# Gate and modulation applied by VectorE, the residual stream put into DRAM before the scatters, and a final norm tile by tile

## The reference

```python
hc, hl = rms_norm(x, norm2) * (1 + sc2) + sh2            # xc and xl, each with its own modulation
xc = xc + g2c * ec_moe(hc, ...)
xl = xl + g2l * ec_moe(hl, ...)
y_prompt, y_sample = rms_norm(xc, final_norm), rms_norm(xl, final_norm)

def ec_moe(x, w_router, w_gate, w_up, w_down):
    gate, idx = top_k(softmax(x @ w_router, over experts), cap)   # 64 latent + 16 context rows per expert
    xs = x[idx]
    y = (silu(xs @ w_gate) * (xs @ w_up)) @ w_down * gate
    return zeros.at[idx].add(y)
```

## Time and profile before

| what | us |
|---|---|
| timed runs | 1527.20, 1529.37, 1529.86; median 1529.37 |
| profiled execution, whole | 1521.83 |
| its span | 1520.0 |
| busy in the span | TensorE 1286.7 (85%), VectorE 890.7 (59%), ScalarE 754.6 (50%), POOL 183.9 (12%) |
| DMA | 322.33 MB, mean 212 GB/s |
| mean granted clock of TensorE | 0.931 of full speed |
| layer 1's expert stage | from about 1158 to 1486 us of the span |

### The profile page before, as it was taken

The page is one execution under the profiler, slowest core; times in us unless marked ns, Lnnn a source line. Parts: engine busy times, 40 slices in busy tenths (PEclk is TensorE's granted clock), DMA queues, the critical chain, the costliest instruction groups (busy, mean ns, idle before and its releaser), DMA issues.

```text
span 1520.0 us, 18235 instructions
## 1 busy us (share of the span) xinstructions
PE 1286.7 (85%) x7585; PEld 929.3 (61%) x7585; DVE 890.7 (59%) x1011; ACT 754.6 (50%) x876; POOL 183.9 (12%) x120
## 2 busy tenths in 40 slices
PE   5699978897679999999669998999953999899990
PEld 3579746795346555556449994668833655555650
DVE  2521367524668878778364352553257688778874
ACT  2321226613357777777243213553144677677762
POOL 1000010010012222211020000000101012222111
PEclk9879989998789999999779999899987999999995
DMA  6731056004699999999862311003054799999984
GB/s 237 236 111 56 28 198 221 2 28 176 231 311 338 364 361 365 363 360 356 285 194 84 97 61 53 2 1 112 2 230 139 275 361 364 360 350 364 369 288 147
DMA packets 98695, 322.33 MB, mean 212 GB/s; under 512 B 6239, under 2 KB 29998, under 8 KB 82230
## 3 DMA queue, kind: packets, MB, share of 16 engines
q1 hardware_dynamic: 86230, 278.39, 50.6%
q0 software_dynamic: 10272, 34.92, 8.6%
q10 hardware_dynamic: 2112, 7.87, 1.3%
HBM read 297.35 MB, written 23.81 MB: 211 GB/s over the span
## 4 chain that ended last, share of the span: by engine, by line
PE 50%; DMA 19%; DVE 16%; ACT 13%; issue 2%; DVEq 0%; ACTq 0%
PE psum L779 47%; DMA stage<-in_moe_w_gate 11%; DVE w_lo L1697 8%; ACT w_hi L1611 5%; ACT arena L1536 3%; DMA stage<-in_moe_w_up 2%; DMA stage<-in_w_mod 2%; DVE arena L1966 2%; ACT arena L1634 1%; DMA arena<-in_x_prompt 1%; DMA arena<-acc_dram 1%; ACT arena L1317 1%; DMA h_dram<-arena 1%; DMA stage<-in_ev_w_in 1%; DVE arena L1729 1%
## 5 line engine op out<-in xcount | busy, mean ns | idle before, releaser
L1697 DVE TENSOR_TENSOR w_lo<-stage,w_hi 128x2048 fp32r<-128x2048 f32 (+1 forms) x216 | 491.5, 2281 | 247.1 <-ACT w_hi L1611 139.9
L1611 ACT ACTIVATE w_hi<-stage 128x2048 fp32r<-128x2048 f32 x192 | 366.7, 1913 | 122.0 <-DMA stage<-in_moe_w_gate 58.1
L779 PE MATMUL psum<-w_hi,h_hi 128*80 128x512 f32 (+1 forms) x848 | 332.5, 392 | 55.1 <-DVE w_lo L1697 34.6
L779 PE MATMUL psum<-w_lo,h_hi 128*80 128x512 f32 (+1 forms) x848 | 326.6, 385 | 0.0
L779 PE MATMUL psum<-w_hi,h_lo 128*80 128x512 f32 (+1 forms) x848 | 326.5, 385 | 0.0
L779 PE MATMUL psum<-h_hi,w_hi 128*128 128x320 f32 x672 | 211.7, 315 | 4.2 <-DVE h_lo L1741 4.2
L779 PEld LDWEIGHTS psum<-w_hi,h_hi 128*80 128x80 f32 (+1 forms) x848 | 130.5, 154 | 135.7 <-DVE w_lo L1697 41.2
L779 PE MATMUL psum<-h_lo,w_hi 128*128 128x320 f32 x672 | 210.2, 313 | 0.0
L779 PE MATMUL psum<-h_hi,w_lo 128*128 128x320 f32 x672 | 210.0, 312 | 0.0
L779 PEld LDWEIGHTS psum<-w_hi,h_lo 128*80 128x80 f32 (+1 forms) x848 | 130.5, 154 | 63.9 <-issue 1.8
L779 PEld LDWEIGHTS psum<-w_lo,h_hi 128*80 128x80 f32 (+1 forms) x848 | 131.0, 154 | 53.6 <-issue 1.2
(11 more groups left out here) (224 smaller groups left out, 1218.6 us busy)
## 6 DMA issues: line engine op xcount, KB each, us to landing
stage<-in_moe_w_gate SPq DMA_DIRECT2D x64, 1024.0 KB, 8.9
stage<-in_moe_w_up SPq DMA_DIRECT2D x64, 1024.0 KB, 9.1
stage<-in_moe_w_down SPq DMA_DIRECT2D x64, 1024.0 KB, 6.6
stage<-in_w_mod SPq DMA_DIRECT2D x48, 1024.0 KB, 7.7
stage<-in_ev_w_in SPq DMA_DIRECT2D x7, 1024.0 KB, 9.4
stage<-in_od_w_in SPq DMA_DIRECT2D x7, 1024.0 KB, 7.7
acc_dram<-arena POOLq DMA_DIRECT2D x2, 2560.0 KB, 13.6
h_dram<-arena ACTq DMA_DIRECT2D x10, 512.0 KB, 3.0
```

The source lines that it names most:

```text
L779: return pe.matmul(o, w, x, start=first, stop=last, skip_group_check=True)
L1611: nc.scalar.activation(split_slot(w_hi, q0), stage[:, PIECE * (p0 % SLOTS):PIECE * (p0 % SLOTS) + PIECE], ACT.Copy)\
L1697: return nc.vector.tensor_tensor(dst, src, hi.bitcast(F32), ALU.subtract)
```

## The change

1. `acc_dram` of layer 1 is no longer cleared. ScalarE stores each `x_out` tile into it, and scatter 0 waits for these five stores.
2. TensorE turns the g2 block (128x16) once, ScalarE copies it and stores it to `gate_dram`, and POOL loads it back as rows: 64 partitions with the latent row, 16 with the context row. POOL also loads `final_norm` onto 128 partitions. Diagonals, spread matmuls and their evacuations go.
3. `rows_out` of layer 1 is VectorE's: one operation multiplies the 80x1024 PSUM result by the gate column and by the g2 row. It stands behind the split of u1, ahead of `hidden_split`; in the last expert behind d0 (expert 14) and at the end (expert 15).
4. At the end SP, not POOL, loads the five tiles, which are now already the sum. ScalarE squares tile t+1 before it makes the root of tile t; VectorE makes mean, Newton step and scaling tile by tile.

```diff
@@ plan_psum
         if L == LAYERS - 1:
+            one("gate rows", "act")
             for t in range(NT):
                 one(("x out", t), "act", 2)
...
-            for b in range(6):
-                one(("spread", b), "act")
@@ SyncE
+            sp.wait_ge(scattered, 16 * E * LAYERS)
+            for t in range(NT):
+                sp.dma_start(acc_out[t], acc_dram[LAYERS - 1][P * t:P * t + P, :]).then_inc(acc_out_in[t], 16)
             for t in range(NT):
                 sp.wait_ge(y_done, t + 1)
@@ GpSimd
-                    for layer in range(LAYERS):
-                        clear(layer)
-                    pool.wait_ge(zero_out, 16 * LAYERS)
+                    clear(0)
+                    pool.wait_ge(zero_out, 16)
...
+                if L == LAYERS - 1:
+                    emptied(pool, ("x out", NT - 1))
+                    pool.dma_start(gain_rows.rearrange("q (k p) -> q k p", k=KD),
+                                   a["final_norm"].rearrange("(o k p) -> o k p", o=1, p=P).to_broadcast([P, KD, P])).then_inc(gain_rows_in, 16)
+                    pool.wait_ge(gate_turned_out, 16)
+                    for rows, g in ((slice(0, CAP_L), 0), (slice(CAP_L, CAP), 1)):
+                        pool.dma_start(gate_rows[rows, :].rearrange("q (k p) -> q k p", k=KD),
+                                       gate_dram[:, g, :].rearrange("(o k) p -> o k p", o=1).to_broadcast([rows.stop - rows.start, KD, P]))\
+                            .then_inc(gate_rows_in, 16)
                 emptied(pool, (L, "gates"))
...
                     pool.wait_ge(y_ready, E * L + e + 1)
+                    if e == 0 and L == LAYERS - 1:
+                        pool.wait_ge(x_stored, 16 * NT)
...
-            for t in range(NT):
-                pool.dma_start(acc_out[t], acc_dram[LAYERS - 1][P * t:P * t + P, :]).then_inc(acc_out_in[t], 16)
@@ TensorE
                 if L == LAYERS - 1:
-
+                    emptied(pe, ("mod turned", LAYERS * MODS - 1))
+                    begin("gate rows")
+                    pe.transpose(bank("gate rows")[0:2 * KD, 0:P], mod_blocks_of(L, 5), ident).then_inc(psum_full, 1)
...
-                    pe.wait_ge(gain_diag_ready, 1)
-                    pe.wait_ge(gate_diag_ready, 1)
-                    for b in range(6):
-                        begin(("spread", b))
...
-                    emptied(pe, ("spread", 5))
-
+                    emptied(pe, ("x out", NT - 1))
@@ ScalarE
                 if L == LAYERS - 1:
+                    act.wait_ge(new_out, 16 * 4)
+                    evacuate("gate rows", gate_turned, bank("gate rows")[0:2 * KD, 0:P])
+                    emptied(act, "gate rows")
+                    act.dma_start(gate_dram.rearrange("k g p -> (k g) p"), gate_turned).then_inc(gate_turned_out, 16)
                     for t in range(NT):
                         evacuate(("x out", t), x_out[t], pair(("x out", t), n=D))
+                        emptied(act, ("x out", t))
+                        act.dma_start(acc_dram[L][P * t:P * t + P, :], x_out[t]).then_inc(x_stored, 16)
...
-                if L == LAYERS - 1:
-                    for b in range(6):
-                        evacuate(("spread", b), spread[:, 512 * b:512 * b + 512], bank(("spread", b)), scale=float(D))
...
                 def rows_out(e):
 
+                    if L == LAYERS - 1:
+                        return
...
+            def root_out_of(t):
+
+                act.wait_ge(mean_ready, t + 1)
+                nc.scalar.activation(root_out[:, t:t + 1], squares_out[:, t:t + 1], ACT.Ln).then_inc(log_done, 1)
+                logs[0] += 1
+                act.wait_ge(log_done, logs[0])
+                nc.scalar.activation(root_out[:, t:t + 1], root_out[:, t:t + 1], ACT.Exp, scale=-0.5).then_inc(root_done, 1)
+
             for t in range(NT):
...
+                act.wait_ge(acc_out_in[t], 16)
+                nc.scalar.activation(x_out[t], acc_out[t], ACT.Square, accum_out=squares_out[:, t:t + 1]).then_inc(x_squared, 1)
+                if t:
+                    root_out_of(t - 1)
+            root_out_of(NT - 1)
@@ VectorE
-                if L == LAYERS - 1:
-                    dve.wait_ge(roped, 8)
-                    for k in range(KD):
-                        ins = nc.vector.tensor_scalar(gain_diag[:, P * k:P * k + P], ident, cols[:, R_FIN + k:R_FIN + k + 1], None, ALU.mult)
...
-                            ins = nc.vector.tensor_scalar(gate_diag[:, at:at + P], ident, mod[:, L, 5, k, g:g + 1], None, ALU.mult)
...
+                def rows_out(e):
+
+                    if L < LAYERS - 1:
+                        return
+                    dve.wait_ge(moe_used, piece_number(e, "d1", 6 * n0 + 1))
+                    if e == 0:
+                        dve.wait_ge(gate_rows_in, 32)
+                    if e >= 2:
+                        dve.wait_ge(scattered, 16 * (n0 + e - 1))
+                    nc.vector.scalar_tensor_tensor(ysb[e % 2].rearrange("p (b n) -> p b n", b=2), psum[0:CAP, 6:8, :], gates[:, e:e + 1],
+                                                   gate_rows.rearrange("p (b n) -> p b n", b=2), ALU.mult, ALU.mult).then_inc(y_ready, 1)
+
                 def step(e, more=True):
                     expert_split(plus(e, 1), "u0")
                     expert_split(plus(e, 1), "u1")
+                    if e:
+                        rows_out(e - 1)
                     hidden_split(e)
...
+            dve.wait_ge(gain_rows_in, 16)
             for t in range(NT):
...
+                mean, root = squares_out[:, t:t + 1], root_out[:, t:t + 1]
+                dve.wait_ge(x_squared, t + 1)
+                nc.vector.tensor_scalar(mean, mean, 1.0 / D, EPS, ALU.mult, ALU.add).then_inc(mean_ready, 1)
+                roots[0] += 1
+                dve.wait_ge(root_done, roots[0])
+                newton(mean, root)
+                nc.vector.scalar_tensor_tensor(x_out[t], acc_out[t], root, gain_rows, ALU.mult, ALU.mult).then_inc(y_done, 1)
```

More of the change, by code:

```diff
@@ L471, in trunk @@
         squares_out, root_out = rowmax, rowsum
-        spread = xT_[:, 0:3 * D]
-        gate_diag, gain_diag = arena[:, 4096:4096 + 2 * D], cs[:, :]
+        gate_rows, gain_rows = xT_[0:CAP, 0:D], xT_[:, D:2 * D]
+        gate_turned = small[0:2 * KD, 0:P]
         consts_in, rows_in, x_in, router_in, sel_in, zeroed, zero_out = (
@@ L496, in trunk @@
         h_out = [sem(f"h_out{s}") for s in range(2)]
[L497 removed]
+        gate_turned_out, gate_rows_in, gain_rows_in, x_stored = (
+            sem(n) for n in ("gate_turned_out", "gate_rows_in", "gain_rows_in", "x_stored"))
         acc_out_in = [sem(f"acc_out_in{t}") for t in range(NT)]
@@ L1627, in rows_out @@
                 def rows_out(e):
+                    if L == LAYERS - 1:
+                        return
                     act.wait_ge(moe_used, piece_number(e, "d1", 6 * n0 + 1))
[L1630 to L1634 removed]
+                    if e >= 2:
+                        act.wait_ge(scattered, 16 * (n0 + e - 1))
+                    nc.scalar.activation(ysb[e % 2].rearrange("p (b n) -> p b n", b=2), psum[0:CAP, 6:8, :], ACT.Copy, scale=gates[:, e:e + 1])\
                         .then_inc(y_ready, 1)
@@ L2112, in _ @@
                 expert_split(E - 1, "d0")
+                rows_out(E - 2)
                 hidden_split(E - 1)
                 expert_split(E - 1, "d1")
+                rows_out(E - 1)
                 if L + 1 < LAYERS:
```

45 lines of the change are left out of this document (6 added, 39 removed).

## The result

Four runs of the changed kernel took 1511.96, 1512.96, 1504.87 and 1505.74 us, median 1508.85; four runs of the kernel before, on the same chip, have a median of 1529.45. The ratio is 0.9877, 95% interval 0.9845 to 0.9909: 18.8 us less (13.9 to 23.7). The forecast was 1513.6 in a range from 1507 to 1523. The profiled execution is one of the longer two, 1511.96 with a span of 1510.1, so the two traces show only 9.9 us of it. I take these apart first; what is missing comes at the end of the experiments. One execution of the kernel before, of 4370 us, stands apart from all its others (1515.6 to 1531.1) and is left out throughout.

A forecast was written before the change was run, and what follows sets the result against it. The weight stream (DMA 1.00 busy at 355 GB/s) was taken to bound the experts, TensorE just under it. Start −9.5, scaling 0, last expert +0.2 and +0.15, tail −6.7 made −15.8 from 1529.4: 1513.6 us, range 1507 to 1523.

The forecast's parts named there:

- The start: Layer 1's slots to first expert matmul: 9.4 us instead of 19.7, 10.3 gained, 9.5 net of slower first 36 matmuls.
- The yardstick from layer 0: Layer 0 starts the same experts without a spread, 9.4 us from slots to first matmul; taken for layer 1.
- What was put ahead of the gather: Ahead of gather 0, ScalarE's extra copy and issues and POOL's three broadcast loads were to cost 0.
- Rival 1: Layer 1's start: broadcasts hold up gather 0, TensorE starts 9 us later than forecast; gain 6.8, 1522.6 us; chance 0.10.
- So I put 0 on it: Expert stage: VectorE's row scaling, 1.25 us per expert, fits into its 1.59 us gap and costs 0.
- the forecast's own sign: First expert matmul to last scaling should take 306.9 + 1 us; over 310 means rival 2 is at work.
- rival 2: Expert stage: rows_out delays release of weight slots, 21.8 us paid, 6 us slower, 1535.4; decides from 1.0 per expert; chance 0.08.
- My argument from the DMA share: Expert stage: DMA engines 1.00 busy, so bandwidth, not free slots, limits the weight stream; held against rival 2.
- The last expert: End of the expert stage: scaling expert 14 ahead of h_lo costs +0.2 us, the slower final scaling +0.15.
- The tail: Last scatter's landing to end: 21.7 us instead of 28.4, 6.7 less, with SP loads and tile-by-tile work 2.5 apart.
- Rival 3: Tail: loads land together, as late as 7.6 us, squares begin 4.5 us later; gain 11.3, 1518.1 us; chance 0.06.
- The sum: Whole kernel: −9.5 + 0 + 0.2 + 0.15 − 6.7 = −15.8 us; span 1504.2, execution 1506.0, median 1513.6.

The follow-up runs named there:

- start_alone: Kernel before with only layer 1's spread replaced by broadcast rows (1.5 MB); scaling on ScalarE and tail as before; median 1515.76 us beside 1525.61, ratio 0.9924.
- after_again: The changed kernel run once more, nothing altered; four runs, median 1508.61 us, ratio 0.988 to the kernel before.
- scale_twice: Changed kernel with VectorE's scaling of the rows issued twice in each expert of layer 1; median 1521.52 us, ratio 0.998 to the kernel before.
- scale_on_scalar: Changed kernel with layer 1's scaling back on ScalarE, by the gate alone, g2 multiplication left out; median 1506.14 us, ratio 0.9858 to the kernel before.
- multiply_on_pool: Changed kernel with ScalarE scaling by the gate and POOL multiplying by the g2 row before each scatter; median 1523.18 us, ratio 0.998 to the kernel before.
- one_root: Changed kernel with one mean, root and Newton step for all five tiles of the last norm; median 1506.22 us, ratio 0.9897 to the kernel before.

## Why the prediction was right

The median came out 4.8 us below 1513.6, inside the range, on the side of "faster".

*The start: right.* Slots to the first matmul 9.32 us, forecast 9.4; gained 10.4, forecast 10.3. The yardstick from layer 0 held because nothing new came onto that chain. Gather 0's instruction took 0.99 us, forecast 0.99, after 3.05 to 3.06 in the three traces of the kernel before; start_alone, which changes the start alone, shows that the change of the start is enough for the gain. The first 36 matmuls took 10.40 us, a loss of 0.4 where I said 0.8.

*What was put ahead of the gather: right, with larger margins than thought.* ScalarE's copies ended at 1151.86 in front of a table load of 1.28, and it waited for TensorE afterwards. POOL's three issues took 0.55 to 0.73 us each, and were over at 1154.0, 2.1 us before gather 0. The broadcasts landed after 5.5, 5.8 and 5.9 us, forecast about 5. Gather 0's transposes began 4.25 us after its issue, sooner than the 6.1 of layer 0 that I took, and on the chain h_lo follows the third split at once. Rival 1 is out: even 1.5 MB did not hold the gather up.

*rows_out: the step that failed is "So I put 0 on it".* Its duration was right, 1.27 against 1.25. The placement in the gap was not. Timeline of VectorE in the kernel before, between the two rows:

```profile
1354.05 0.48 DVE L1697 TENSOR_TENSOR h_lo<-psum,h_hi 128x320 fp32r<-128x320 f32 x1
1354.48 2.29 DVE L1697 TENSOR_TENSOR w_lo<-stage,w_hi 128x2048 fp32r<-128x2048 f32 x1
1356.97 2.29 DVE L1697 TENSOR_TENSOR w_lo<-stage,w_hi 128x2048 fp32r<-128x2048 f32 x1 [0.20 <-ACT w_hi L1611]
```

The gap of 1.59 us stands ahead of g0's split, and it is there behind all fourteen experts that have a g0 to follow (1.29 to 2.2 us). But h_lo and the splits of d0 and d1 come before it, with 0.2 us of idle time between them here. A gap can only take in the delay of what stands behind it. Whatever delay the insert brings reaches these three first, and I asked only whether VectorE had caught up afterwards, not what the two splits let go. Timeline of VectorE in an expert of the kernel after:

```profile
1304.58 2.29 DVE L1713 TENSOR_TENSOR w_lo<-stage,w_hi 128x2048 fp32r<-128x2048 f32 x1 [2.66 <-ACT w_hi L1621]
1306.79 1.27 DVE L2099 SCALAR_TENSOR_TENSOR arena<-psum,arena,xT 80x1024 f32<-80x1024 f32 x1
1307.99 0.47 DVE L1713 TENSOR_TENSOR h_lo<-psum,h_hi 128x320 fp32r<-128x320 f32 x1
1308.39 4.70 DVE L1713 TENSOR_TENSOR w_lo<-stage,w_hi 128x2048 fp32r<-128x2048 f32 x2
...
1319.44 2.29 DVE L1713 TENSOR_TENSOR w_lo<-stage,w_hi 128x2048 fp32r<-128x2048 f32 x1 [0.63 <-ACT w_hi L1621]
```

Behind the scaling VectorE runs from 1306.8 to 1318.8 without a pause: the gap ahead of g0 is used up. The idle time has moved to where u0 and u1 are waited for, 2.66 us here, which is of no use to what stands behind the insert. The price is some 5.7 us in the stage. By the forecast's own sign, over 310 us from the first expert matmul to the last scaling, rival 2 was at work: 317.2 us in this trace and 312.5 in after_again. It is rival 2 in its mechanism but at less than a third of its price, 0.36 us per expert against the 1.0 from which it decides; scale_twice, at 0.8 to 1.1 more per expert, is what the full price looks like. My argument from the DMA share did not hold, since it is too blunt: 0.36 us in 19.2 are 2% of the stage. From 1180 to 1440 us the share is 1.00 and 0.99 in start_alone and scale_on_scalar, 0.98 or 0.99 in the seven traces with one scaling on VectorE, and only in scale_twice and multiply_on_pool does it fall to 0.96. That the cost comes with VectorE's doing the scaling, and grows when it does so twice, is shown; that it is passed on by the slots of d0 and d1 is read from the waits above.

*The last expert: small, as said.* Issue to landing of the last scatter 5.23 instead of 5.06 us; the final scaling 1.28 instead of 1.12. The 0.2 us for expert 14 is not isolated by any run.

*The tail: right.* 21.0 us, forecast 21.7. Tile 0's square started at 1492.69, 3.6 us after the scatter's landing (forecast 3.3); the chain then waited for tile 1, landed 4.87 us after it (4.8); the period is 2.43 (2.50); from the last store to the end 3.0 us, where I had 3.4. Rival 3 is out, the tiles landed from 3.5 to 6.9 us after issue. What the forecast did not say is how little the tile-by-tile part brings: one_root lost only 0.5 us, since each tile pays its own chain of root and Newton step.

*The sum: right by two errors that cancel.* I left out 5.7 us of cost in the middle, and the timed runs contain some 6 us of gain that no changed stage shows. That the median fell inside the range is, for this part, luck: by the traces alone the change is worth 12.4 us where I had 15.8. The profiled execution, 1511.96, was 6.0 us above the 1506.0 that I gave for it.

## What to carry to other kernels

A gap behind an insert pays only for what stands behind the gap. Before an insert is put at nothing, list the operations between its place and the gap, and what each of them lets go (here the slots of two weight pieces); and double the insert once, since the second one shows how much room the first has left. To price a start, take the same stage in another layer that lacks the removed work; this gave 9.4 for 9.3 us. And in a pass that is repeated per tile, issue the small operation that another engine waits for ahead of the large one (2.43 us per tile became 1.84).

## What was unexpected in the hardware

- **POOL's scatter instruction stretches beside VectorE's unbroken work.** The indirect scatter's instruction took 2.2 to 2.3 us on average when ScalarE scaled the rows and released it, and 3.3 to 4.0 when VectorE did (4.8 when twice); in multiply_on_pool, released by POOL's own multiplication, it took 3.0. Single ones, timeline of POOL, then VectorE's split behind its next pause, kernel after:

```profile
1225.76 1.43 POOL L770 DMA_INDIRECT acc_dram<-arena  x1 [11.57 <-DVE arena L2099]
...
1246.32 5.82 POOL L770 DMA_INDIRECT acc_dram<-arena  x1 [16.66 <-DVE arena L2099]
...
1251.93 2.29 DVE L1713 TENSOR_TENSOR w_lo<-stage,w_hi 128x2048 fp32r<-128x2048 f32 x1 [0.36 <-ACT w_hi L1621]
```

  It is now released by VectorE's scaling and so starts just as the splits behind it do. Where VectorE ran on, up to 1251.57, the instruction ended 0.57 us after that; where VectorE paused 0.1 us after the instruction's start, it took 1.43. That is the likeliest reason for POOL's 22 us more. scale_on_scalar takes it away together with the scaling, so these runs can't say for certain whether it has a share in the 5.7 us. Its length and L1−L0 do not go together, though (4.0 us at +1.6, 3.5 at −1.3, 3.0 at +14.5), and POOL idled 11.6 to 16.7 us ahead of these two, so it had room for it.
- **VectorE's split is slower beside POOL's arithmetic:** 2.29 us became 3.94. POOL's 80x1024 took 3.44 us on average, where 2.4 had been estimated; no run shows it undisturbed.
- **Three broadcasts in 512-byte pieces**, 0.8 MB in all, landed in 5.5 to 5.9 us with only the last stores of x beside them, and of three that make 1.5 MB the first in 4.4, the others in 6.8 and 7.7; the 512 KB that took 11.3 us at the kernel's start had the first weights beside them.
- **The same code ran at a granted clock from 0.81 to 0.97** in one stretch of 74 us in fourteen executions, with 12 us between the earliest and the latest arrival at 200 us: as much as the terms that this change is made of.
